# Attention group A: the third score term as two 64-row products on different row halves, in place of two 128-row products

## The reference, cut to what matters

```
def gqa_axial_mixer(qa, ka, va, q_gain, k_gain, tabs):
    ...
    q = apply_axial_rope(rmsnorm(qa.reshape(B, S, N_HEADS_A, HEAD_DIM), q_gain), tabs)
    k = apply_axial_rope(rmsnorm(ka.reshape(B, S, N_KV_A, HEAD_DIM), k_gain), tabs)
    ...
        logits = jnp.einsum('bqkgd,bskd->bkgqs', qg, k)
        p = softmax_f32(logits, scale, v.dtype)
        o = jnp.einsum('bkgqs,bskd->bqkgd', p, v)
...
for l in range(DEPTH):
    ...
    o_a = gqa_axial_mixer(qa, ka, va, q_norm_a[l], k_norm_a[l], tabs_a)
    o_b = mla_mixer(cq, ckv, kr, ...)
    o_c = diff_alibi_mixer(qc, kc, vc, ...)
    x = x + jnp.concatenate([o_a, o_b, o_c], axis=-1) @ w_out[l]
    h = rmsnorm(x, norm_ffn[l])
    x = x + conv_gated_mlp(h, w_up[l], conv_w[l], conv_b[l], w_down[l])
return rmsnorm(x, final_norm)
```

## Time and profile before

| | us |
|---|---|
| median of 3 runs | 3010.93 (3009.47 to 3011.11) |
| the profiled execution, whole | 3007.72 |
| its span, first to last instruction | 3005.9 |
| mean granted TensorE clock | 0.99 of full |
| busy: PE / PEld / DVE / ACT / POOL | 2899.8 / 2316.6 / 2010.4 / 1313.2 / 474.9 |

### The profile page before, as it was taken

The page is one execution under the profiler, slowest core; times in us unless marked ns, Lnnn a source line. Parts: engine busy times, 40 slices in busy tenths (PEclk is TensorE's granted clock), DMA queues, the critical chain, the costliest instruction groups (busy, mean ns, idle before and its releaser), DMA issues.

```text
span 3005.9 us, 36862 instructions
## 1 busy us (share of the span) xinstructions
PE 2899.8 (96%) x13560; PEld 2316.6 (77%) x13560; DVE 2010.4 (67%) x2316; ACT 1313.2 (44%) x1826; POOL 474.9 (16%) x250
## 2 busy tenths in 40 slices
PE   6999889999999999999999998899999999999998
PEld 4777656888778888888877785578887888888887
DVE  5877887992366655555678778889716555556555
ACT  3236788993322221222233287889823212222223
POOL 3111232223300000000131123322341000000002
PEclk8999999999999999999999999999999999999999
DMA  4455333323111211111135643234312111111101
GB/s 180 144 176 139 71 71 84 84 63 112 43 56 46 67 42 42 56 42 42 40 132 180 173 105 71 64 85 91 112 43 70 43 42 56 42 42 56 56 28 56
DMA packets 236372, 236.48 MB, mean 79 GB/s; under 512 B 59488, under 2 KB 199520, under 8 KB 236256
## 3 DMA queue, kind: packets, MB, share of 16 engines
q1 hardware_dynamic: 236256, 234.94, 27.4%
HBM read 184.04 MB, written 50.86 MB: 78 GB/s over the span
## 4 chain that ended last, share of the span: by engine, by line
PE 85%; DVE 8%; issue 4%; ACT 2%; DMA 1%; SPq 0%; POOL 0%; DVEq 0%; ACTq 0%
PE ps L1743 29%; PE ps L1758 16%; PE ps L1503 16%; PE ps L1593 8%; PE ps L1665 6%; PE ps L1631 3%; PE ps L1632 3%; DVE ps L1218 2%; PE ps L1627 2%; PE ps L1728 1%; PE ps L1529 1%; DVE xgl L1118 1%; PE ps L1678 1%; DVE prob L1287 1%; DVE rstd L1360 0%
## 5 line engine op out<-in xcount | busy, mean ns | idle before, releaser
L1593 PE MATMUL ps<-stack 128*128 128x512 f32 (+1 forms) x1152 | 347.3, 419 | 42.1 <-ACT prob L907 19.1
L1409 DVE TENSOR_TENSOR xT<-ps,xT 128x512 f32<-128x512 f32 x352 | 241.9, 691 | 214.4 <-PE ps L1758 214.2
L1665 PEld LDWEIGHTS ps<-cst,prob 128*128 128x128 f32 x2048 | 255.3, 142 | 90.2 <-issue 20.4
L1593 PEld LDWEIGHTS ps<-stack 128*128 128x128 f32 (+1 forms) x1152 | 206.9, 191 | 152.5 <-ACT prob L907 50.5
L1665 PE MATMUL ps<-cst,prob 128*128 128x128 f32 x2048 | 311.5, 275 | 7.8 <-issue 4.1
L907 ACT ACTIVATE prob<-ps,nmx 128x1024 f32<-128x1024 f32 x256 | 284.6, 1112 | 22.8 <-PE ps L1665 12.3
L1323 DVE TENSOR_TENSOR ptl<-ps,pth 128x512 fp32r<-128x512 f32 x384 | 259.1, 685 | 47.3 <-ACT pth L969 42.7
L1374 DVE SCALAR_TENSOR_TENSOR cv<-u,vec,cv 128x1024 f32<-128x1024 f32 x176 | 225.8, 1283 | 88.4 <-ACT cv L1046 78.2
L1058 ACT ACTIVATE ah<-cv 128x1024 fp32r<-128x1024 f32 x44 | 46.7, 1061 | 533.2 <-DVE cv L1387 533.2
L1743 PE MATMUL ps<-xgh,w0h 128*128 128x512 f32 x704 | 274.1, 389 | 2.6 <-ACT sq L1038 2.6
L1743 PE MATMUL ps<-xgl,w0h 128*128 128x512 f32 x704 | 273.9, 389 | 0.0
(11 more groups left out here) (225 smaller groups left out, 5587.8 us busy)
## 6 DMA issues: line engine op xcount, KB each, us to landing
wraw<-in_w_up SPq DMA_DIRECT2D x88, 512.0 KB, 4.7
draw<-in_w_down SPq DMA_DIRECT2D x22, 1024.0 KB, 4.9
stack<-ka_d SPq DMA_DIRECT2D x64, 256.0 KB, 5.4
wraw<-in_w_in SPq DMA_DIRECT2D x30, 512.0 KB, 4.0
vst<-v_d SPq DMA_DIRECT2D x48, 256.0 KB, 3.8
x_d<-xT SPq DMA_DIRECT2D x2, 4096.0 KB, 17.7
wraw<-in_w_out SPq DMA_DIRECT2D x16, 512.0 KB, 5.5
stack<-qc_d SPq DMA_DIRECT2D x64, 128.0 KB, 3.6
```

What stands on the lines that cost most here:

```text
L1409: ins = dve.tensor_tensor(xs, ps[:, 4 + j % 4, :], xs, ALU.add)
L1593: ins = pe.matmul(score_banks(i)[:, kh, :], st[q][0:rows, c0:c0 + P], st[k][0:rows, kh * HALF:(kh + 1) * HALF], start=n == 0, stop=n == le ...
L1665: ins = pe.transpose(ps[:, 4 + s % 2, m * P:(m + 1) * P], prob[:, b, m, s * P:(s + 1) * P], ident)
```

## The change

The term (qh + ql) kl is replaced with qh kl alone, so the small product ql kl is no longer computed. Its contraction has 64 rows. The two matmuls are laid on different halves of the array: keys 0 to 511 on rows 0 to 63, keys 512 to 1023 on rows 64 to 127. For that, tile 3 now holds qh on both halves, and tile 2 holds kl of the first key half on partitions 0 to 63 and of the second on 64 to 127. A head of group A has 8 loads where it had 6.

```
-LOADS = {"A": 6, "B": 8, "C": 16}
+LOADS = {"A": 8, "B": 8, "C": 16}
...
                     if group == "A":
                         for s in range(2):
                             sp.dma_start(st[0][s * HD:(s + 1) * HD, :].bitcast(F32), qa_d[s, h * HD:(h + 1) * HD, :]).then_inc(full, 16)
-                            for c in range(2):
-                                kv = h // (NA // NKV)
-                                sp.dma_start(st[1 + s][c * HD:(c + 1) * HD, :].bitcast(F32), ka_d[s, kv * HD:(kv + 1) * HD, :]).then_inc(full, 16)
+                        kv = h // (NA // NKV)
+                        for c in range(2):
+                            rows, cols = slice(c * HD, (c + 1) * HD), slice(c * HALF, (c + 1) * HALF)
+                            sp.dma_start(st[1][rows, :].bitcast(F32), ka_d[0, kv * HD:(kv + 1) * HD, :]).then_inc(full, 16)
+                            sp.dma_start(st[2][rows, cols].bitcast(F32), ka_d[1, kv * HD:(kv + 1) * HD, cols]).then_inc(full, 16)
+                            sp.dma_start(st[3][rows, :].bitcast(F32), qa_d[0, h * HD:(h + 1) * HD, :]).then_inc(full, 16)
...
                     if x["group"] == "A":
-                        rows, terms = P, ((0, 1), (0, 2))
+                        rows, terms = P, ((0, 1),)
...
                     for n, (q, k) in enumerate(terms):
                         for kh in range(2):
                             ins = pe.matmul(score_banks(i)[:, kh, :], st[q][0:rows, c0:c0 + P], st[k][0:rows, kh * HALF:(kh + 1) * HALF],
-                                            start=n == 0, stop=n == len(terms) - 1)
+                                            start=n == 0, stop=x["group"] != "A" and n == len(terms) - 1)
+                    if x["group"] == "A":
+                        for kh in range(2):
+                            rows = slice(kh * HD, (kh + 1) * HD)
+                            ins = pe.matmul(score_banks(i)[:, kh, :], st[3][rows, c0:c0 + P], st[2][rows, kh * HALF:(kh + 1) * HALF], start=False, stop=True)
                     ins.then_inc(scores_done, 1)
```

## The result

The changed kernel takes 3025.03 us (median of 5 runs, 3021.96 to 3029.82) against 3009.47 us (5 runs, 3006.39 to 3011.11) for the kernel before: ratio 1.0056, 95% interval 1.0043 to 1.0069.

The account below looks back on a forecast made before the run. PE was taken to bound group A. Per item 0.40 us for two steps less 0.12 overlap gives +0.28; times 126 is 35.3 us on 3007.72, 3043.0, plus 3.2 to the median: 3046 us, range 3030 to 3063.

Parts of the forecast that it names:

- What bounds group A: Group A: PE sets the end, busy for all 11.33 us of a unit; DVE and ACT work stays hidden.
- the 0.8 us in hand: Group A: DVE and ACT have 0.8 us slack per unit, so shortening PE pays for only that much.
- the loads: Group A: eight loads per head instead of six are issued over 22 us before use and cost nothing.
- The step down: Score item on PE: going from 128-row to 64-row matmuls costs 0.20 us extra, with the weight loader idle.
- The overlap of the pair: Two 64-row matmuls of an item: they run together, second starting 0.11 us after the first, saving 0.12 us.
- loads side by side: Rival for the 64-row pair: both halves load and multiply together, +0.17 us per item, 21.4 us, 3032 us; chance 0.08.
- The step back: End of a score item on PE: returning from 64-row to 128-row matmuls costs 0.20 us extra.
- The sum: 126 score items of group A at +0.28 us each make 35.3 us more PE time on the path.

Follow-up runs that it names:

- experiment 5: Third term left out altogether, two 128-row products per item and no step, against the kernel before: 2986.6 us, ratio 0.9926.
- experiment 4: Kernel before with two more loads per head of group A, products as before, against the kernel before: 3010.13 us, ratio 1.0001.
- Experiment 1: Changed kernel with both 64-row products on rows 0 to 63, one behind the other: 3054.66 us, ratio 1.0146 to the kernel before.
- experiment 2: Changed kernel without the 64-row product of the second key half, three products per item: 3021.64 us, ratio 1.0041 to the kernel before.
- Experiment 3: Changed kernel with the 64-row pair ahead of the two 128-row products: 3028.85 us, 1.0061 to the kernel before; run again 3031.91 us, 1.0076.
- second profile of the changed kernel: Changed kernel run again unaltered, on one chip with the kernel that puts the 64-row pair first: 3022.81 us, ratio 1.0044 to the kernel before.
- experiment 7: Items in twos, one step down and back per two, against kernel before: 1.0307; maxima and exponentials spread 1.0291, also exponentials ahead 1.0268, spread with 128-row third products 1.0311.
- experiment 6: Changed kernel with the pair of 64-row products issued twice in each item: 3050.45 us, ratio 1.0137 to the kernel before.

## Why the prediction was wrong, point by point

**What bounds group A** was right. PE had no idle time in the unit before and has none after, and taking work from PE (experiment 5) gains until DVE and ACT hold it at 10.68 us per unit: of the 0.8 us in hand 0.65 could be had. DVE and ACT stayed hidden, and so did the loads (experiment 4).

**The step down** was right: 0.33 us from the last 128-row start to the 64-row load, 0.20 us over the steady pace, as in the earlier trace rows.

**The overlap of the pair** is the step that failed: "their loads go one behind the other through the one loader, 0.11 us apart", 0.12 us saved. The loads start together and the saving is the whole product, 0.23 us; over 126 items this is some 14 of the 20 us by which the sum was too high. I took the middle value because the loads in the earlier trace rows were 0.11 apart, but these were for the same rows. Experiment 1 beside the changed kernel shows both cases, 0.11 on the same rows and 0.00 on different ones, and experiment 2 shows that the second product is free. The right value stood in the prediction as the rival "loads side by side", with a chance of 0.08. By the Trainium skill (TensorE: Matmul & The Clock Gate, Part 3) matmuls on different row tiles start some 4 ns apart. The trace agrees: the two products of a pair start 3 or 4 ns apart in each of the 128 items, in the rows above at 534.74.

**The step back** is the second: I carried 0.20 us from the earlier trace rows, where an fp32r product follows the step. Here a transpose follows, and the step costs 0.15: some 6 us over 126 items. Experiment 3 puts fp32r products there, and the item costs +0.17 instead of +0.12, so it is what follows the step that counts. The next load comes 0.06 us after the first there, not 0.11, which is the size of the difference; that this is its cause was not tested by itself. This error also set the lower end of the range too high: the end of 3030 took 0.40 us for the two steps as fixed and left only the overlap to vary.

**The sum** with both terms as measured is 0.195 + 0.15 - 0.23 = +0.12 us per item, 15 us for 126 items. The medians (15.6 and 14.1 us) agree. The profiles show where it lies. The pairs of layer one, in the first and in the second profile of the changed kernel:

```profile
L1601 PE MATMUL ps<-stack x128: 491/500/502, 490.8 to 682.3; 64*128 64x512 f32 x128
L1601 PE MATMUL ps<-stack x128: 491/500/501, 491.0 to 682.5; 64*128 64x512 f32 x128
```

From the first item to the last go 191.5 us in both. Before it was 184.8 from the first product of the first item to the last product of the last, 184.1 from item to item. Counted from the matmuls just ahead of the first item to those just behind the last, by their starts, the changed kernel loses 7.6 us per layer, 15.2 in all, in both profiles. The whole spans are 18.7 and 15.5 us over before. In the second, the parts outside group A come to 0.3 us net. In the first they come to 3.5, and 3 of these lie where the granted clock is at its lower level, 1.2 GHz, behind the last item of group A. In the changed kernel there are these two stretches (length, busy us of each engine, then the clock):

```profile
693.80:697.40 3.60, 3.60 (x16) 3.19 (x16) 0.99 (x2) 1.01 (x2) 1.27 (x1) 0.53 0.30 123
2175.20:2182.30 7.10, 7.10 (x31) 6.20 (x31) 2.91 (x5) 3.25 (x5) 1.27 (x1) 0.52 0.21 84
```

The same places in the profile of before:

```profile
685.90:689.10 3.20, 3.20 (x29) 2.99 (x27) 1.72 (x3) 1.44 (x4) 1.28 (x1) 1.00 0.77 306
2160.50:2164.10 3.60, 3.60 (x16) 3.00 (x15) 1.38 (x2) 2.08 (x3) 1.12 (x1) 0.53 0.15 58
```

The second profile of the changed kernel has a clock of 1.00 at both places, so I count the 3 us to the single execution; whether the change makes such a fall likelier was not tested.

## What to carry to other kernels

Two half-height products on different row halves cost one product, loads and all, but the step into that mode and out of it cost 0.35 us here, more than the 0.23 us gained. By these figures such a pair can pay only if two or more stand together in one stretch, and the gain that was seen of that is 0.2%, at the edge of what the runs can tell (experiment 7). Bringing them together must not disturb the buffers either: here, with two sets of banks, grouping cost 3%. When a cost is carried from one place of a trace to another, ask what differs: the rows used, and what stands behind the step. Before paying for a smaller term at all, take it out once: the whole third term was worth 0.7%, since DVE and ACT stood right behind PE.

## What the runs showed of the hardware that was not expected

Weight loads for different row halves start within 0.01 us of each other, while on the same rows they are 0.11 us apart (experiment 1). The first load of a transpose after a step is followed by the next load after 0.06 us, that of an fp32r product after 0.11 us, and a step back is 0.05 us cheaper in front of transposes (0.15 us in the changed kernel, 0.20 in experiment 3). One half-height product alone takes the time of two on different halves (0.43 us with its step, experiment 2). Two pairs in a row take 0.67 us, one product's time more than one pair (experiment 6).
